# The last projection of a two-block layer: its weight block sums move into accumulating DMAs, its seven products into another order

## What is computed

```
a   = (a * silu(za)) @ w_att_out
sgo = (sgo * silu(zs)) @ w_sg_out
ga, gs = split(sigmoid(gm + b_merge))
y   = ga * a + gs * sgo
x   = x + y @ w_o
return rmsnorm(x, final_g)
```

## Time and profile before

| | us |
|---|---|
| median of three runs | 1301.88 (1301.75 to 1302.64) |
| the profiled execution | 1301.86 |
| its span | 1300.1 |
| PE busy | 1281.3 (99%) |
| DVE busy | 860.9 (66%) |
| ACT busy | 635.3 (49%) |
| POOL busy | 733.8 (56%) |

### The profile page before, as it was taken

One profiled execution on the slowest core, in us unless ns is written; L12 is line 12 of the kernel. 1 busy time (PEld: TensorE's weight loads), 2 busy tenths in 40 slices (PEclk: granted clock), 3 DMA queues, 4 the chain that ended last, 5 costly groups with the idle time before them and its releaser, 6 DMA issues.

```text
span 1300.1 us, 19911 instructions
## 1 busy us (share of the span) xinstructions
PE 1281.3 (99%) x7696; PEld 1109.2 (85%) x7696; DVE 860.9 (66%) x1269; ACT 635.3 (49%) x1026; POOL 733.8 (56%) x517
## 2 busy tenths in 40 slices
PE   9999999999999999999999999999999999999986
PEld 8877777887888889989988998877778899999865
DVE  3674544556544599448835857766547999995897
ACT  6223534556533565325532546354557456675353
POOL 4463333435454578648856866533433876665965
PEclk9999999999999999999999999999999999999988
DMA  6333151413223333233333334322221333335301
GB/s 206 96 116 105 41 154 45 150 41 110 93 73 98 90 96 108 98 97 98 111 118 94 94 114 138 106 71 79 92 65 65 118 111 98 95 103 175 116 17 65
DMA packets 142266, 128.66 MB, mean 99 GB/s; under 512 B 4512, under 2 KB 134688, under 8 KB 142176
## 3 DMA queue, kind: packets, MB, share of 16 engines
q1 hardware_dynamic: 141824, 127.23, 31.8%
q10 hardware_dynamic: 352, 0.19, 0.1%
HBM read 122.04 MB, written 2.10 MB: 95 GB/s over the span
## 4 chain that ended last, share of the span: by engine, by line
PE 95%; DVE 3%; DMA 1%; ACT 1%; issue 0%; SPq 0%; ACTq 0%; DVEq 0%
PE gemm L886 16%; PE gemm L887 16%; PE gemm L894 16%; PE gemm L1198 9%; PE gemm L1203 9%; PE gemm L1199 9%; PE gemm L910 2%; PE gemm L911 2%; PE gemm L916 2%; PE gemm L943 2%; PE gemm L944 2%; PE gemm L949 2%; PE mix L1324 1%; PE mix L1312 1%; PE mix L1301 1%; DMA xtm<-x 1%
## 5 line engine op out<-in xcount | busy, mean ns | idle before, releaser
L713 POOL TENSOR_TENSOR wlo<-raw,whi 128x512 fp32r<-128x512 f32 x264 | 368.0, 1425 | 278.5 <-ACT whi L1471 259.0
L886 PE MATMUL gemm<-hh,whi 128*128 128x512 f32 x552 | 219.2, 397 | 0.0
L887 PE MATMUL gemm<-hl,whi 128*128 128x512 f32 x552 | 215.3, 390 | 0.0
L741 POOL TENSOR_TENSOR wlo<-raw,whi 128x512 fp32r<-128x512 f32 x108 | 159.6, 1504 | 47.1 <-ACT whi L1680 39.0
L1471 ACT ACTIVATE whi<-raw 128x2048 fp32r<-128x2048 f32 x62 | 118.5, 1911 | 45.4 <-PE gemm L894 26.0
L894 PE MATMUL gemm<-hh,wlo 128*128 128x512 f32 x552 | 138.0, 390 | 0.0
L886 PEld LDWEIGHTS gemm<-hh,whi 128*128 128x128 f32 x552 | 103.6, 188 | 25.5 <-issue 4.0
L1198 PE MATMUL gemm<-hh,whi 128*128 128x256 f32 x496 | 124.7, 284 | 0.0
L1199 PE MATMUL gemm<-hl,whi 128*128 128x256 f32 x496 | 124.3, 283 | 0.0
L887 PEld LDWEIGHTS gemm<-hl,whi 128*128 128x128 f32 x552 | 103.7, 188 | 20.9 <-issue 0.2
L894 PEld LDWEIGHTS gemm<-hh,wlo 128*128 128x128 f32 x552 | 103.2, 188 | 21.2
(11 more groups left out here) (544 smaller groups left out, 3147.7 us busy)
## 6 DMA issues: line engine op xcount, KB each, us to landing
raw<-w_in SPq DMA_DIRECT2D x53, 1024.0 KB, 5.3
raw<-w_gu SPq DMA_DIRECT2D x44, 512.0 KB, 4.9
raw<-w_down SPq DMA_DIRECT2D x16, 512.0 KB, 4.4
raw<-w_o SPq DMA_DIRECT2D x6, 1024.0 KB, 5.1
raw_b<-w_branch SPq DMA_DIRECT2D x16, 256.0 KB, 5.7
raw<-w_ao SPq DMA_DIRECT2D x4, 1024.0 KB, 5.0
raw<-w_so SPq DMA_DIRECT2D x4, 1024.0 KB, 5.0
raw<-w_in SPq DMA_DIRECT2D x7, 512.0 KB, 4.1
```

Source lines behind the costliest of these rows:

```text
L713: last = nc.gpsimd.tensor_tensor(a(wlo), a(raw), as_f32(a(whi)), ALU.subtract)
L741: return nc.gpsimd.tensor_tensor(part_of(wlo, u, b), raw_block(u, f, k), as_f32(part_of(whi, u, b)), sub)
L886: mm(bank[:, :], w, xh[:, k, :], start=(k == 0), stop=False)
L887: mm(bank[:, :], w, xl[:, k, :], start=False, stop=False)
```

## The change

- SP loads w_o's blocks from an array that the host has laid out block by block (`o2_block`), so that each partition's share of a block is one run of 8 KB. Blocks now go to blk_v (two), blk_a (two halves), both raw slots, and, after the last ordinary unit, blk_q and blk_w.
- The sums of blocks are made by eight DMAs that POOL issues with accumulation (`add_block`): the destination in SBUF is added to. Each waits until the one before has landed. All sums have plus signs, and the combinations subtract where that is needed. DVE's block sums and POOL's difference are gone. P3 is now a product with the sum of all four blocks.
- The low part of a block sum is written over it (blk_v_lo, blk_a_lo, blk_q_lo) or over a buffer that has come free.
- PE's order: P1, pair, P5 with a pair inside, pair, P2 with a pair inside, P3, P7, P6, P4. The transposes alternate between B4 and B1, so the first pair waits for the last ordinary tile to be out of PSUM (tile_free), not for P1's copy.
- DVE makes the first late sums before tile 6 and takes P5's low part between these sums and their rests. In its combinations, each takes one operand straight out of PSUM; u2_s and v_s are gone. POOL forms ten sums of kept inputs with p1_s and p5_s, then scales.

```diff
+        def o2_block(k0, f, k=4):
+            return w_o2[k0 // 4, f][:, k0 % 4:k0 % 4 + k]
...
             for f in range(2):
-                sp.dma_start(wa[f][:, :, :], cols(w_o2, f * 512, 512, 0, 4)).then_inc(sem("wT_in"), 16)
+                sp.dma_start(blk_v[f][:, :, :], o2_block(0, f)).then_inc(sem("wT_in"), 16)
...
+            sp.wait_ge(sem("wT_in"), 48)
             for i in range(2):
-                sp.dma_start(w_sum[i][:, :, :], cols(w_o2, 512, 512, 4 + 2 * i, 2)).then_inc(sem("wT_in"), 16)
+                sp.dma_start(blk_a[i][:, :, :], o2_block(4 + 2 * i, 1, 2)).then_inc(sem("wT_in"), 16)
...
+            sp.wait_ge(sem("tile_done"), T_END)
+            sp.wait_ge(sem("wT_in"), 80)
+            sp.dma_start(blk_q[:, :, :], o2_block(0, 1)).then_inc(sem("wT_in"), 16)
+            sp.dma_start(blk_w[R3][:, :, :], o2_block(4, 1)).then_inc(sem("wT_in"), 16)
...
+            def add_block(dst, src):
+                if added[0]:
+                    pool.wait_ge(sem("added"), 16 * added[0])
+                added[0] += 1
+                nc.gpsimd.dma_start(dst, src, accum_op=ALU.add).then_inc(sem("added"), 16)
+
+            raw_r2 = wide(raw, R2)[:, :, :]
+            pool.wait_ge(sem("wT_in"), 48)
+            add_block(blk_v[1][:, :, :], o2_block(0, 0))
             rests(n_gs + 5, n_gs + 6)
-            block_rest(L_P1, wa[0])
+            pool.wait_ge(sem("wT_in"), 80)
+            for h in range(2):
+                add_block(blk_a[h][:, :, :], o2_block(2 * h, 1, 2))
+            block_rest(L_P1)
             rests(n_gs + 6, N_UNITS)
-            pool.wait_ge(sem("s_made"), 3 * N_SEVEN + 1)
-            for k in range(4):
-                last = nc.gpsimd.tensor_tensor(wa[1][:, k, :], wa[0][:, k, :], wa[1][:, k, :], sub)
-            last.then_inc(sem("s3_made"), 1)
-            block_rest(L_P2, wb[0])
-            block_rest(L_P7, wa[1])
-            block_rest(L_P4, wb[1])
+            pool.wait_ge(sem(f"raw_in{R2}"), raw_count(n_o2))
+            add_block(raw_r2, o2_block(0, 0))
+            block_rest(L_P7)
+            add_block(raw_r2, o2_block(0, 1))
+            block_rest(L_P2)
+            add_block(raw_r2, o2_block(4, 1))
+            pool.wait_ge(sem("wT_in"), 112)
+            add_block(blk_q[:, :, :], o2_block(4, 1))
+            add_block(blk_q[:, :, :], o2_block(0, 0))
+            block_rest(L_P4)
...
                 if i < 2:
-                    pe.wait_ge(sem("p1_read"), N_SEVEN + 1 + i)
+                    pe.wait_ge(sem("tile_free"), T_END)
+                elif i < 4:
+                    pe.wait_ge(sem("p1_read"), N_SEVEN + i - 1)
                 else:
-                    pe.wait_ge(sem("o_copied"), i - 1)
+                    pe.wait_ge(sem("o_copied"), i - 3)
...
+            last_product(L_P1, B1, hh[:, 0:4, left], hl[:, 0:4, left])
+            turn_pair(0)()
             pe.wait_ge(sem("t_lo"), 13)
+            last_product(L_P5, B2, u_hi[:, 0], o_lo[0], turn_pair(2))
+            turn_pair(4)()
             pe.wait_ge(sem("y2_lo"), KD)
+            last_product(L_P2, B3, hh[:, 4:8, left], hl[:, 4:8, left], turn_pair(6))
+            pe.wait_ge(sem("o_copied"), 6)
+            last_product(L_P3, B4, hh[:, 4:8, right], hl[:, 4:8, right])
...
+            last_product(L_P7, B1, u_hi[:, 2], o_lo[2])
             pe.wait_ge(sem("p1_read"), N_SEVEN + 4)
+            last_product(L_P6, B2, u_hi[:, 1], o_lo[1])
+            pe.wait_ge(sem("c_sum"), C_END + 2)
+            last_product(L_P4, B3, hh[:, 0:4, right], hl[:, 0:4, right])
...
             gated_rest(5)
+            late_sums(0)
             block_rest(L_P5)
-            block_sum(1, in_sum, lambda ks: wa[0][:, ks, :], ALU.subtract)
+            late_rests(0)
             gated_tile(6)
             gated_rest(6)
             gated_tile(7)
-            late_sums(0)
             gated_rest(7)
-            late_rests(0)
             late_sums(1)
             late_rests(1)
-            block_rest(L_P6)
...
+            block_rest(L_P3)
...
             for t in range(2):
+                dve.wait_ge(sem("row_pre"), 1 + t)
+                combine(half_of(t, 0), B3[t][:, :], half_of(t, 0), ALU.add, 5 + t)
             for t in range(2):
+                dve.wait_ge(sem("row_pre"), 5 + t)
+                combine(half_of(2 + t, 0), B4[t][:, :], half_of(2 + t, 0), ALU.add, 7 + t)
+            first_squares(slice(0, 2), 2)
+            block_rest(L_P6)
```

More of the change, by code:

```diff
@@ L801, in _, with block_rest @@
             seven_group(SECOND, no_product)
[L802 to L810, removed]
-                for k in range(4):
-                    last = nc.gpsimd.tensor_tensor(low[:, k, :], block[:, k, :], as_f32(high[:, k, :]), sub)
-                last.then_inc(sem("lo_done" if i else "first_block_lo"), 1)
+            def block_rest(i):
+                pool.wait_ge(sem("s_hi"), HIGH_AT[i])
+                for k in range(4):
+                    h, c = k // 2, k % 2
+                    last = nc.gpsimd.tensor_tensor(LOW[i][h][:, c, :], BLOCK[i][h][:, c, :], as_f32(HIGH[i][:, k, :]), sub)
+                last.then_inc(sem("s3_lo"), 1)
@@ L825, in _ @@
+            add_block(raw_r2, o2_block(0, 0))
[7 more added lines that the diff above has]
+            block_rest(L_P4)
             pool.wait_ge(sem("o_copied"), 8)
+            pool.wait_ge(sem("p1_read"), N_SEVEN + 4)
+            tt = nc.gpsimd.tensor_tensor
@@ L826, in _ @@
             for t in range(2):
[L827 to L829 removed]
+                tt(xr[t][:, 0:512], xr[t][:, 0:512], p1_s(t), ALU.add).then_inc(sem("row_pre"), 1)
             for t in range(2):
[L831 to L833 removed]
@@ L834, in _ @@
-                pool.wait_ge(sem("row_pre"), 3 + 2 * t)
-                nc.gpsimd.tensor_tensor(p5_s(t), p5_s(t), xr[2 + t][:, 512:], ALU.add).then_inc(sem("row_pre"), 1)
+                tt(p5_s(t), p1_s(t), p5_s(t), sub).then_inc(sem("row_pre"), 1)
+            for t in range(2):
+                pool.wait_ge(sem("row_pre"), 3 + t)
+                tt(xr[2 + t][:, 0:512], xr[2 + t][:, 0:512], p5_s(t), ALU.add).then_inc(sem("row_pre"), 1)
+            for t in range(2):
+                tt(xr[2 + t][:, 512:], xr[2 + t][:, 512:], p5_s(t), sub).then_inc(sem("row_pre"), 1)
@@ L836, in _ @@
+            for t in range(2):
+                tt(xr[t][:, 512:], xr[t][:, 512:], p1_s(t), sub).then_inc(sem("row_pre"), 1)
             pool.wait_ge(sem("c2_in"), 80)
-            for t, h, count in ((2, 1, 3), (3, 1, 4), (1, 0, 2)):
+            for t, h, count in ((1, 0, 2), (2, 1, 4), (3, 1, 6)):
                 pool.wait_ge(sem("row_sq"), count)
@@ L1417, in last_product @@
                     if t == 0:
-                        pe.wait_ge(sem(low[0]), low[1])
+                        pe.wait_ge(sem(LOW_AT[i][0]), LOW_AT[i][1])
                     for k in range(4):
-                        last = mm(banks[t][:, :], xh[:, k, tok], rest[:, k, :], start=False, stop=(k == 3))
+                        last = mm(banks[t][:, :], xh[:, k, tok], LOW[i][k // 2][:, k % 2, :], start=False, stop=(k == 3))
                     last.then_inc(sem("last_ps"), 1)
@@ L2038, in _ @@
[L2038 removed]
             y2_high(7)
[L2040 to L2047 removed]
+            sum_highs(1)
+            for t in range(2):
+                keep_product(2, p1_s, B1, t)
             keep_input(0)
@@ new lines, in _ @@
+            block_high(L_P3)
+            for t in range(2):
+                keep_product(4, p5_s, B2, t)
+            for i in range(4, 8):
+                keep_input(i)
+            act.wait_ge(sem("added"), 128)
+            block_high(L_P6)
+            square_row(0, 0, 1)
+            square_row(1, 0, 2)
+            square_row(2, 0, 9)
+            square_row(2, 1, 10)
+            row_root(2, 1)
+            square_row(3, 0, 12)
+            square_row(3, 1, 13)
+            row_root(3, 1)
@@ L2995, in _ @@
-            dve.wait_ge(sem("c_sum"), C_END + 6)
-            for t in range(2):
-                dve.wait_ge(sem("row_pre"), 4 + 2 * t)
-                combine(half_of(2 + t, 1), v_s(t), p5_s(t))
-            for t in range(2):
-                last = tt(half_of(t, 1), v_s(t), half_of(t, 1), ALU.add)
-            link(last)
-            combine(half_of(2, 0), B2[0][:, :], half_of(2, 0), 11)
-            first_squares(1, slice(2, 4), 1)
+                dve.wait_ge(sem("row_pre"), 7 + t)
+                combine(half_of(2 + t, 1), half_of(2 + t, 1), B1[t][:, :], ALU.subtract, 9 + t)
```

221 lines of the change are left out of this document (84 added, 137 removed).

## The result

The changed kernel takes 1319.72 us (median of four runs, 1318.93 to 1320.55) against 1302.2 for the one before (also four runs): a ratio of 1.0136, with a 95% interval of 1.0123 to 1.0148, so 17.5 us slower. The profiled execution's span is 1317.1 against 1300.1.

A forecast was written before the change was run, and what follows sets the result against it. The prediction took PE to bound the kernel (95% of the chain). PE's end at 1297.2 plus a tail of 8.5 gave a span of 1305.7, so 1307.5 us, 5.6 slower; range 1294.5 to 1320.

The forecast's parts named there:

- rival 3: Eight adds: accumulating at half rate or worse, issue 1.8, landings 8.5 and 5.1; 1321.4 us, chance 0.14.
- step 2: DVE before the transposes: tile 7's multiplication late, slowed by eight POOL instructions; PE waits 6.1, with 1.5 of slow clock.
- Step 1: Ahead of P1's low part: add 1 costs nothing; adds 2 and 3 idle PE 3.3 before unit 101's low products.
- D: POOL's delay from adds 2 and 3 after unit 100's rests: issue, landing, issue, 6.1 us.
- A: Landing time of a 1 MB add, between 5.1 and 11.0, taken as 6.8 us.
- A': Landing time of a 512 KB add, between 3.4 and 5.1, taken as 4.3 us.
- X: Time of DVE's multiplication of tile 7, which frees the banks for the transposes: 1253.9.
- Step 3: Chain of adds to P6's low part on DVE: PE waits 3.7 for it and ends at 1297.2.
- Step 4: Tail after PE's end: 8.5 instead of 11.7 us, about 7.1 unhindered.
- Step 5: 8 KB weight rows, fg2b's later load, in-place low parts, B3 freed after two combinations: no effect.
- Rival 1: Adds at plain loads' price, issue 0.34, landings 5.1 and 3.4: span 1298.7, 1300.5 us, no change; chance 0.24.
- Rival 2: DVE's crowding by POOL before the transposes falls away: 1296.6 with half gone, 1292.7 with all; chance 0.26.

The follow-up runs named there:

- Experiment 3: Changed kernel with adds 2 and 3 moved behind P1's and unit 101's low parts: 1312.91 us.
- Experiment 1: Changed kernel with POOL's eight adding DMAs as plain copies, same buffers and waits, sums of blocks not made: 1307.47 us.
- experiment 2: Changed kernel without any DMA by POOL, sums of blocks and the waits on them left out: 1295.86 us.
- Experiment 4: Changed kernel with a one-column write by POOL and a wait for it behind each DMA issue: 1314.68 us.
- own3_nogap: Changed kernel with adds moved, separate semaphores for adds, P6's low part early, ACT and PE reordered, but no gaps behind POOL's DMAs: 1310.66 us.

## Why the prediction was right or wrong

The direction and the three places where PE waits were right; the size, 5.6 for 17.5, was not, and the middle wait had another cause than the one given. The forecast's own part ended at 1314; that 1319.7 lies inside the whole range, by 0.3, is luck, as its upper end was only set just short of rival 3.

Of the 11.4 us between the predicted span and the measured one (1305.7, 1317.1), 4.2 come ahead of P1 (2.0 more idleness, 2.2 of slow clock), 0.8 before P6's low part is wanted, 5.8 from the wait for it and 1.7 from the slow clock behind it; step 2 adds 0.3, and the tail gives 1.5 back.

- **Issue of POOL's DMAs, 0.9:** 0.86 to 1.00. Right. Rival 3's way by which the issue is held up behind a running DVE instruction is not seen; it is DVE that was held up.
- **Step 1 failed at "costs nothing, covered unless it takes over 8 us".** Add 1 took 12.6, its neighbours in the queues being SP's loads of w_sg_out. Adds 2 and 3 started at 1211.6, not 1207.8, and the second of them waited 5.5. So PE stood still 5.3 and not 3.3 ahead of unit 101's low products, and the clock, taken as nothing, cost 2.2 more. The working held for D (6.1 predicted; from 1211.55 to 1218.51 it is 7.0) and for the slack of 2.8; it was the one edit that was costed as hidden. Experiment 3 moved the adds away and got 6.0 back.
- **The landings were the mis-sized term.** A = 6.8 was 8.0 in an empty queue, 10.4 (the median of three, two of them beside loads of 1 MB) to 12.6 in company; A' = 4.3 was 5.7. The second megabyte was taken at half of what it costs to load, 1.7, and costs 2.9 even with nothing beside it; and the adds also ran beside loads of SP's, for which only one place of the eight was charged. Add 8 went out at 1277.6 and landed at 1285.6, predicted 1269.3 and 1276.1. Experiment 1 prices the adding itself, with the one lock-out that goes with it, at 11.4 us of span.
- **Step 2 had the right number for a wrong reason.** 6.1 was predicted ahead of the transposes, and 6.3 came, behind tile 7's multiplication; X was 1258.4 (PE starts at 1258.51) in place of 1253.9. The mechanism given, POOL's eight instructions at 0.97 each, would act in experiment 2 also, and there is no wait there; two instructions of 5.2 and 5.4 did it. Experiment 4 shortens both and the wait goes with them. Only because POOL's DMAs stand directly ahead of its runs is it there at all. The second pair's wait, 2.0, was 1.2.
- **Step 3, P6's low part:** a wait of 3.7 predicted, 9.5 measured. The chain was as told (last add, P4's low part, sums, B4's combinations, low part), but the last add went out 8.3 later, and PE, itself late, wanted the low part at 1289.8 and not 1284.5. POOL's sums went at 1.4 a piece against 1.3; then a multiplication of 128x2 numbers, not in the prediction's list but for "0.9", was locked out for 5.46.
- **Step 4, the tail:** 8.5 predicted, 7.1 unhindered; measured 7.0. Right. The combinations had piled up while PE waited, and were done before P4.
- **Step 5, nothing:** no wait of these runs goes back to it. But "nearly empty" queues, put against rival 3, became busy for 0.93 of the stretch, with the change's own loads and adds in them; an argument from a stretch of the kernel before doesn't hold for what the change itself puts there.
- **Rival 1's plain prices** gave 1298.7 of span; the kernel with plain transfers has 1305.7. The lock-out still stands ahead of two of its waits, and its landings beside loads are 7.0 to 7.9 and not 5.1; no run splits the two. **Rival 2** (times of 1292.7 to 1296.6, no crowding) is what experiment 2 shows in number, 1295.9, but with no DMA at all, not with cheap ones, and with DVE and POOL still slowing each other. **Rival 3** (landings of 8.5 and 5.1) is nearest in time, 1321.4 for 1319.7, with its chance of 0.14; its landings are near the ones measured in an empty queue (8.0 and 5.7), and its S of 5.9 near the 5.3. It had the issue wrong (1.8) and didn't have the lock-out, so that it comes so close is in part luck.

The Trainium skill, "SBUF — State Buffer", section "SBUF: two separate sides", says of the port pair that DVE and GpSimd share that whichever instruction starts first holds it for that whole instruction. The kernel before agrees (four of POOL's in 6.4 to 7.1, DVE's in 1.7, in turn). Behind an issue the runs show more than that: DVE got no turn between POOL's instructions, at up to eight in a row (11.01 us).

## What to carry to other kernels

A sum moved from an engine to DMA isn't free: count its landing at what the queue carries at that moment, with the change's own loads in it (here 8.0 alone and 10.4 to 12.6 in company for 1 MB), and never put it ahead of work that has less slack than that. Keep POOL's DMA issues away from its runs of instructions, or let POOL rest for a moment behind each; here a write of one column and a wait for it gave 4.2 us in one order and 11.8 in another, by one run each. And test order and mechanism apart: the new order without any block sums was worth 6.0 us all along, and only a kernel without the DMAs showed it.

## What the runs showed of the hardware that was not expected

- **The lock-out:** behind a DMA that POOL issues, adding or plain, 128 KB or 1 MB, a run of POOL's instructions that follows with no rest keeps DVE's instructions with operands in SBUF out for the whole of the run: 5.1 to 6.1 us for four, 11.0 for eight. One on 128x2 and, in `own3_nogap`, two on 128x1024 asked amid a longer run and stood still to its end (5.46 and 13.91 with their own work). POOL's four then take 4.9 to 5.4 and not 6.4 to 7.1. Instructions with one operand out of PSUM go on at 0.69. A write of one column with a rest of about 0.1 us behind it ends it (experiment 4), and so did bare rests: 1.0 in experiment 1, and 0.4 in experiment 3, where DVE beside the four rests behind add 2 took 1.41 and 1.77. In `own3_nogap`, with no rest at that place, the first of these two took 3.19.
- **Adding:** 1 MB from an array into SBUF lands 8.0 us after the issue, plain 5.1, with nothing beside it; 512 KB 5.7 and 4.7 in the changed kernel and in experiment 1. The issue on POOL takes 0.86 to 1.00 adding, 0.53 to 0.72 plain.
- **Loads beside it:** the load of 1 MB by SP (blk_w) that ran beside an add landed after 9.0 us in the changed kernel and after 9.7 beside plain transfers (experiment 1), so the adding itself isn't seen in it.
